# A stick-breaking attention stage with four softplus slots, its mask in the scores and its rounding on VectorE

## What is computed

```python
z = jnp.einsum("bhtd,bhsd->bhts", qb, kb) * scale
causal = s_idx < t_idx
log_not = jnp.where(causal, jax.nn.log_sigmoid(-z), 0.0)
tail = lax.cumsum(log_not, axis=3, reverse=True) - log_not
log_a = jax.nn.log_sigmoid(z) + tail
a = jnp.where(causal, jnp.exp(log_a), 0.0)
outs.append(jnp.einsum("bhts,bhsd->bhtd", a, vb))
```

## Time and profile before

| what | us |
|---|---|
| median of the three runs | 2361.65 |
| the profiled execution's own time | 2363.2 |
| its span, first to last instruction | 2361.4 |
| around the span | 1.8 |
| TensorE busy | 2258.7 |
| VectorE busy | 976.8 |
| ScalarE busy | 841.4 |
| GpSimd busy | 975.1 |

### The profile page before, as it was taken

How to read it: one execution, slowest core, us unless ns; L and a number is a source line. 1 busy time by engine, 2 the same in 40 slices (tenths; PEclk the granted TensorE clock), 3 DMA queues, 4 the chain that set the end, 5 groups by cost and what they waited for, 6 DMA issues and landing times.

```text
span 2361.4 us, 28298 instructions
## 1 busy us (share of the span) xinstructions
PE 2258.7 (96%) x10366; PEld 1781.8 (75%) x10366; DVE 976.8 (41%) x1433; ACT 841.4 (36%) x1410; POOL 975.1 (41%) x435
## 2 busy tenths in 40 slices
PE   8999999998889899999999999999999789999997
PEld 6888887874446688888777888888877458888886
DVE  3112347356674511134675421124552663211344
ACT  4222235323663422223443332222342763322222
POOL 4444444551002544444453354444443433544442
PEclk9999999998889999999999999999999989999999
DMA  5222332331001132223232232222222002322222
GB/s 184 89 106 89 107 107 89 125 125 36 1 1 38 70 107 89 107 89 118 78 107 72 90 107 91 104 89 107 80 95 76 19 1 72 122 92 93 103 89 71
DMA packets 29801, 202.67 MB, mean 86 GB/s; under 512 B 3360, under 2 KB 4000, under 8 KB 6048
## 3 DMA queue, kind: packets, MB, share of 16 engines
q1 hardware_dynamic: 28800, 198.55, 23.9%
q10 hardware_dynamic: 928, 3.14, 0.4%
HBM read 198.54 MB, written 2.10 MB: 85 GB/s over the span
## 4 chain that ended last, share of the span: by engine, by line
PE 87%; DVE 5%; ACT 4%; issue 2%; POOL 1%; ACTq 0%; DVEq 0%; POOLq 0%
PE PS L947 26%; PE PS L949 26%; PE PS L948 26%; PE PS L1270 1%; PE PS L1239 1%; DVE ACC L1430 1%; PE PS L1374 1%; PE PS L1198 1%; PE PS L1362 1%; DVE TMP L1510 1%; DVE NMAX L1662 1%; POOL X L471 1%; PE PS L1018 1%; PE PS L1094 0%; DVE PB L1681 0%
## 5 line engine op out<-in xcount | busy, mean ns | idle before, releaser
L446 POOL TENSOR_TENSOR WL<-RAW,WH 128x1024 fp32r<-128x1024 f32 x368 | 908.8, 2473 | 1276.0 <-ACT WH L512 1276.0
L947 PE MATMUL PS<-XH,WH 128*128 128x512 f32 (+1 forms) x2200 | 866.9, 394 | 30.4 <-DVE XL L1422 20.9
L949 PE MATMUL PS<-XH,WL 128*128 128x512 f32 (+1 forms) x2200 | 853.4, 388 | 0.0
L948 PE MATMUL PS<-XL,WH 128*128 128x512 f32 (+1 forms) x2200 | 853.1, 388 | 0.0
L512 ACT ACTIVATE WH<-RAW 128x1024 fp32r<-128x1024 f32 x368 | 388.1, 1059 | 1262.2 <-PE PS L949 1218.3
L947 PEld LDWEIGHTS PS<-XH,WH 128*128 128x128 f32 x2200 | 415.3, 189 | 126.6 <-issue 27.5
L948 PEld LDWEIGHTS PS<-XL,WH 128*128 128x128 f32 x2200 | 415.7, 189 | 85.8 <-issue 4.1
L949 PEld LDWEIGHTS PS<-XH,WL 128*128 128x128 f32 x2200 | 415.1, 189 | 84.8
L949 PE MATMUL PS<-HH,WL 128*128 128x512 f32 x672 | 261.7, 389 | 0.0
L948 PE MATMUL PS<-HL,WH 128*128 128x512 f32 x672 | 261.7, 389 | 0.0
L947 PE MATMUL PS<-HH,WH 128*128 128x512 f32 x672 | 261.7, 389 | 0.0
(11 more groups left out here) (194 smaller groups left out, 1639.3 us busy)
## 6 DMA issues: line engine op xcount, KB each, us to landing
RAW<-wstream SPq DMA_DIRECT2D x183, 1024.0 KB, 4.8
X<-xT SPq DMA_DIRECT2D x4, 512.0 KB, 9.4
WORK<-memT ACTq DMA_DIRECT2D x2, 1024.0 KB, 5.5
outT<-WORK SPq DMA_DIRECT2D x8, 256.0 KB, 2.1
RAW<-wstream SPq DMA_DIRECT2D x2, 512.0 KB, 6.5
PB<-WORK ACTq DMA_DIRECT2D x8, 127.8 KB, 2.4
CST<-consts SPq DMA_DIRECT2D x1, 912.0 KB, 12.1
WORK<-constsb SPq DMA_DIRECT2D x1, 256.0 KB, 12.7
```

Source lines behind the costliest of these rows:

```text
L446: pool.tensor_tensor(WL[:, s, :, :].rearrange("p a b -> p (a b)"), RAW[:, s, :], WH[:, s, :, :].rearrange("p a b -> p (a b)").bitcast(F), ...
L947: pe.matmul(o, wh, xh, start=start, stop=False)
L948: pe.matmul(o, wh, xl, start=False, stop=False)
L949: return pe.matmul(o, wl, xh, start=False, stop=stop)
```

## The change

The additive mask of the diagonal block moves from the end of the tail to just behind the scores of the pair (`sb_strict`), and VectorE's multiplication with the mask goes. The softplus is -1e30 clipped, so 0, where masked. The softplus has four slots in place of two, two of them in a new SBUF tensor `LT`. The rounding leaves ScalarE: VectorE makes the same maximum a second time, now written as fp32r into `XH`, two steps behind the clip; the unrounded maximum stays one step behind. The steps of every other round put their `XH` and `XL` columns at another place of the slot (`sb_cols`: 128 or 256 columns on for the two narrow widths), so that the rounding waits for a tail of one or two rounds before instead of the tail two steps before.

```diff
@@ -278,6 +278,7 @@
         VC = sb("VC", [32, P])
         EPSB = sb("EPSB", [P, 1])
         RSTDM = sb("RSTDM", [P, M])
+        LT = sb("LT", [P, 2, S])
         PS = ctx.enter_context(nc.psum_tensor("PS", [P, 8, S], F))
 
 
@@ -287,6 +288,7 @@
         V_WIN = W[:, 19, :].rearrange("p (t c) -> p t c", t=NT)
         V_SB = W[:, 14:20, :].rearrange("p a b -> p (a b)").rearrange("p (t c) -> p t c", t=NT)
         ASLOT = [PB[:, 2, :], PB[:, 3, :], W[:, 20, :], W[:, 21, :]]
+        LSLOT = [PB[:, 0, :], PB[:, 1, :], LT[:, 0, :], LT[:, 1, :]]
         ESLOT = [PT[:, 0, :], PT[:, 1, :], TMP[:, 0, :], TMP[:, 1, :]]
 
         PSLOT = [PB[:, m, :] for m in range(4)] + [W[:, 20, :], W[:, 21, :], Y0[:, :], ACC[:, :]]
@@ -376,6 +378,11 @@
         sums_ready = sem("sums_ready")
         out_ready, stored = sem("out_ready"), sem("stored")
 
+        def sb_cols(t, width):
+
+            at = (t // 8 % 2) * (P, 2 * P, 0, 0)[t % 8 // 2]
+            return slice(at, at + width)
+
         SBSTEPS = [(2 * c + r, j) for c in range(6) for j in range(NT - 1, -1, -1) for r in range(2)]
 
         def y_wait(eng, part, k):
@@ -478,7 +485,8 @@
                 for t, (h, j) in enumerate(SBSTEPS):
                     w = S - j * P
                     pool.wait_ge(sb_hi, t + 1)
-                    pool.tensor_tensor(XL[:, t % 8, 0:w], PB[:, t % 2, 0:w], XH[:, t % 8, 0:w].bitcast(F),
+                    pool.tensor_tensor(XL[:, t % 8, sb_cols(t, w)], LSLOT[t % 4][:, 0:w],
+                                       XH[:, t % 8, sb_cols(t, w)].bitcast(F),
                                        ALU.subtract).then_inc(sb_lo, 1)
 
 
@@ -906,14 +914,6 @@
                 act.wait_ge(sb_exp, t + 1)
                 act.activation(e, e, ACT.Ln, bias=1.0).then_inc(sb_ln, 1)
 
-            def sb_round(t):
-
-                w = S - SBSTEPS[t][1] * P
-                act.wait_ge(sb_l, t + 1)
-                if t >= 8:
-                    act.wait_ge(sb_tri, t - 1)
-                act.activation(XH[:, t % 8, 0:w], PB[:, t % 2, 0:w], ACT.Copy).then_inc(sb_hi, 1)
-
             def sb_weights(t):
                 w = S - SBSTEPS[t][1] * P
                 act.wait_ge(sb_tri, t + 1)
@@ -926,8 +926,6 @@
                     sb_weights(t - LAG_T)
                 if t < n:
                     sb_exp_ln(t)
-                if 1 <= t <= n:
-                    sb_round(t - 1)
             round_o(OUT_ORDER["outB"], lambda k: act.wait_ge(sb_o, k + 1) if k < 6 else
                     act.wait_ge(o_taken, 10 + k - 5))
             refill("outB", KC - 1)
@@ -1360,7 +1358,11 @@
                     pe.wait_ge(sb_a, (t | 1) - SBANKS + 1)
                 r = slice(DH * (h % 2), DH * (h % 2) + DH)
                 pe.matmul(PS[:, t % SBANKS, 0:S - j * P], W[r, 8 + h // 2, j * P:(j + 1) * P],
-                          Q[r, h // 2, j * P:S], start=True, stop=True).then_inc(sb_qk, 1)
+                          Q[r, h // 2, j * P:S], start=True, stop=False, skip_group_check=True)
+
+            def sb_strict(t):
+                pe.matmul(PS[:, t % SBANKS, 0:P], IDB, CSB[:, B_STRICT:B_STRICT + P], start=False, stop=False,
+                          skip_group_check=True).then_inc(sb_qk, 1)
 
             def sb_tail(t):
 
@@ -1371,10 +1373,9 @@
                 for n in range(NT - j):
                     col, width, m = n * P, w - n * P, SUMS[:, 1 if n == 0 else 0, :]
                     for part in (XH, XL):
-                        pe.matmul(bank[:, col:w], m, part[:, (t - 2 * n) % 8, 0:width], start=False,
-                                  stop=False, skip_group_check=True)
-                pe.matmul(bank[:, 0:P], IDB, CSB[:, B_STRICT:B_STRICT + P], start=False, stop=True,
-                          skip_group_check=True).then_inc(sb_tri, 1)
+                        mm = pe.matmul(bank[:, col:w], m, part[:, (t - 2 * n) % 8, sb_cols(t - 2 * n, width)], start=False,
+                                       stop=n == NT - j - 1 and part is XL, skip_group_check=True)
+                mm.then_inc(sb_tri, 1)
 
             def sb_values(t):
                 h, j = SBSTEPS[t]
@@ -1392,6 +1393,8 @@
                 if t < n:
                     sb_scores(t)
                     sb_scores(t + 1)
+                    sb_strict(t)
+                    sb_strict(t + 1)
                 if 0 <= t - LAG_T < n:
                     sb_tail(t - LAG_T)
                     sb_tail(t + 1 - LAG_T)
@@ -1803,7 +1806,7 @@
                 w = S - SBSTEPS[t][1] * P
                 dve.wait_ge(sb_qk, t + 1)
                 if t >= 4:
-                    dve.wait_ge(sb_l, t - 3)
+                    dve.wait_ge(sb_hi, t - 3)
                 dve.tensor_scalar(ESLOT[t % 4][:, 0:w], PS[:, t % SBANKS, 0:w], SPW, None,
                                   ALU.min).then_inc(sb_clip, 1)
 
@@ -1811,15 +1814,27 @@
 
                 w = S - SBSTEPS[t][1] * P
                 dve.wait_ge(sb_ln, t + 1)
-                if t >= 2:
-                    dve.wait_ge(sb_lo, t - 1)
-                lt = PB[:, t % 2, :]
-                chain(dve.tensor_tensor(lt[:, 0:w], ESLOT[t % 4][:, 0:w], PS[:, t % SBANKS, 0:w], ALU.max))
-                dve.tensor_tensor(lt[:, 0:P], lt[:, 0:P], CST[:, K_MASK:K_MASK + P], ALU.mult).then_inc(sb_l, 1)
+                if t >= 4:
+                    dve.wait_ge(sb_lo, t - 3)
+                lt = LSLOT[t % 4]
+                dve.tensor_tensor(lt[:, 0:w], ESLOT[t % 4][:, 0:w], PS[:, t % SBANKS, 0:w],
+                                  ALU.max).then_inc(sb_l, 1)
+
+            def sb_round(t):
+
+                w = S - SBSTEPS[t][1] * P
+                dve.wait_ge(sb_ln, t + 1)
+                c = t // 8 - (t % 8 < 4)
+                if c > 0:
+                    dve.wait_ge(sb_tri, 8 * c - 1 + t % 2)
+                dve.tensor_tensor(XH[:, t % 8, sb_cols(t, w)], ESLOT[t % 4][:, 0:w], PS[:, t % SBANKS, 0:w],
+                                  ALU.max).then_inc(sb_hi, 1)
 
             for t in range(n + LAG_V + 3):
                 if t < n:
                     sb_clip_(t)
+                if 2 <= t <= n + 1:
+                    sb_round(t - 2)
                 if 1 <= t <= n:
                     sb_soft(t - 1)
                 d = t - LAG_V - 1
```

## The result

The change made the kernel faster: 2343.16 us median of 8 runs (2338.72 to 2351.60) against 2360.43 us median of 8 for the kernel before. The ratio is 0.9929, 95% interval 0.9915 to 0.9943, so 16.8 us (13.5 to 20.1) came off where 11.2 were forecast. The time lies in the forecast range, 2341.5 to 2358.5. The kernel timed a second time beside the last experiments had 2346.73 us and a ratio of 0.9921 (0.9907 to 0.9935). Among the experiments one execution, of e6_scalar_no_turns, took 5978.67 us; its ratio leaves it out, and its cause is not known.

What follows compares the result with a forecast made beforehand. Bound: a loop of waits between TensorE's scores and first tail and ScalarE's queue. Saving 1.86 us a round, times 6, 11.2 us: profiled 2363.2 to 2352.0, and 2350.5 because that execution lay 1.55 above the median; range 2341.5 to 2358.5.

Steps and rivals of the forecast that it cites:

- Part 1: ScalarE's queue: two roundings leave each period, saving 2.96 us per round; the rounding's wait for the tail adds nothing.
- Part 2: TensorE: two mask matmuls before the first tail where one stood at its end, costing 0.24 us per round.
- Part 3: VectorE: mask multiplication (26.3 us) goes, second maxima (23 us) come at the first's price; SBUF operands judged dearer.
- Part 4: GpSimd's low part, behind VectorE's fuller queue, reaches the second tail of width 384 late by 0.72 us per round.
- Part 5: ScalarE's exp waits for a later clip in the period of the 384 scores: late by 0.14 us.
- Sum per round: Net saving of the stage per round: 2.96 - 0.24 - 0.72 - 0.14 = 1.86 us.
- Ends: Beginning and end of the stage together lose roundings from their chains, put at one more round's saving.
- Rival A: Denser work keeps TensorE's clock up, and the low part's lateness may not come: 2342.5 us; chance 0.2.
- B: VectorE's queue becomes the bound, second maxima held while GpSimd works; 7 us less saving, 2357.5 us; chance 0.16.
- C: TensorE's clock falls for most of the stage, costing 22.5 us: 2373 us; chance 0.04.
- D: Roundings were not on the loop; another wait takes over, gaining at most 2 us: 2360 us; chance 0.05.
- The signs: Profile marks of a right forecast: forecast periods, ScalarE back to back, stage about 96 us for 107, rest of span unchanged.

Runs made afterwards that it cites:

- e6_scalar_no_turns: e1_round_scalar without the turned columns and their looser wait, so ScalarE's rounding waits for the tail two steps before; 2360.17 us, ratio 0.9992.
- e7_copy_later: The changed kernel with VectorE's copy of a round's values one step later, behind the pair's second rounding; 2339.74 us, one execution.
- e5_mask_only: The kernel before with only the mask added behind the scores and VectorE's mask multiplication gone; 2360.09 us, ratio 0.9987.
- e1_round_scalar: The changed kernel with the rounding back on ScalarE, as a Copy from the softplus slot, keeping the looser wait; 2349.63 us, ratio 0.9936.
- after_again: The changed kernel itself, unedited, timed and profiled again beside e11_all; 2346.73 us, ratio 0.9921.
- e3_two_slots: The changed kernel with two softplus slots in place of four; 2344.80 us, one execution.
- e11_all: The changed kernel with rounding as VectorE's copy from SBUF, values' copy one step later, both weights of a pair before exp and ln; 2338.83 us, ratio 0.9894.

## Why the prediction was right, and where it was off

The forecast mechanism is what happened: a loop of TensorE's first tail and ScalarE's queue sets the periods, and it became shorter by the roundings that left it. One step failed without spoiling the number: the wait of the rounding for the tail, which the prediction put at nothing, was worth about half of what it booked under the roundings. By its steps:

*Part 1, two roundings leave each period, 2.96 us a round.* As the sum it holds (its first term is 1.07 and not 1.06, which changes nothing): 2.30 us came off net, and 0.5 to 0.6 were given back as lateness. As an account of what the roundings cost it fails. I wrote that the wait of the rounding for the tail was worth nothing beyond its queue time. In fact that wait is what put the first rounding on the loop: without it ScalarE does the first one in idle time, 15.32 us a round instead of 16.86. Taking the roundings off ScalarE is worth the rest, 0.77 us net, or 1.28 if the lateness that the move brings is taken out as well (15.32 to the 14.04 of e7_copy_later). The looser wait and the move both take the same first rounding off the loop, so they don't add, and the turns add nothing to the move (14.55 with and without).

*Part 2, masks ahead of the tail, 0.24 us a round.* Mis-sized: 0.0 net of the multiplication, from e5_mask_only, and 0.02 a period by the rows of e6_scalar_no_turns.

*Part 3, second maximum at the price of the first.* Right: 0.278, 0.410, 0.545 and 0.678 us for the four widths. That the SBUF form would be dearer was wrong for the copy: the row of 0.547 us read for it is an average over multiplications that were free (0.29) and held.

*Part 4, the low part late by 0.72 us in the period of the 128 scores.* Right in place and cause, a little too large: 0.49 us of wait; when the cause goes the period shortens by 0.6 and the round by 0.5. The low part ended 5.69 us after the 512 scores (5.94 forecast), and the second tail was ready for it at about 5.26 (5.22). VectorE's first clip came earlier than I had put it: in the changed kernel's period of the 512 scores, which start at 1867.75 us, it stood at 1.33 us, not 1.49:

```profile
1869.08 0.69 DVE L1810 TENSOR_SCALAR TMP<-PS 128x512 f32<-128x512 f32 x1 [0.74 <-PE PS L1364]
```

*Part 5, exp late by 0.14 in the period of the 384 scores.* That period lost 0.52 us of the 0.63 of its roundings, so about 0.1. Right.

*Sum per round.* 1.86 forecast, 2.30 to 2.38 measured (16.85 to 16.94 less 14.55). The excess is part 2 (0.24) and part 4 (about 0.2, from 0.72 to 0.51 net). Of the 15.39 us of the five rounds 12.3 are this, with the shorter first one: five full-clock rounds before are 84.3 to 84.7 us, after they took 72.17. I had put 9.3.

*Ends.* 1.86 forecast, 0.41 + 1.41 = 1.82 measured. The forecast was a round's saving taken over and not worked out, so the agreement is in part luck.

*Rival A, the clock.* The remaining 3.1 us of the 15.39 are rounds of the kernel before that the clock made longer: 87.56 us in place of 84.5. In the changed kernel the clock was 1.00 there, which is the sign that the prediction had set for A, and 2343.16 us lies nearer to A's 2342.5 than to 2350.5. But the clock is only 3.1 us of the 7: A came true in part, beside the forecast, and not through the absence of the lateness. What kept the clock is open. Over 1835 to 1915 us it was 0.97 to 1.00 in the nine profiles with a round of 14.6 us or less, 0.94 in e1_round_scalar (15.32), and below that it does not follow the round: 0.89 before, 0.87 with the mask alone, 0.86 with the turns alone (15.88), 0.84 in e6_scalar_no_turns. Those are single executions, nothing was done to the clock by itself, and the dips in after_again and e3_two_slots (rounds of 15.99 and 16.01 us) show that the changed kernel isn't free of them. The page "TensorE: Matmul & The Clock Gate" of the Trainium skill, Part 1, says that activity releases the throttle; the step from 0.84 to 0.89 up to 0.97 to 1.00 agrees with it in direction, the order within the slower four does not show it.

*Rivals B, C and D.* B: no second maximum was held, and between the waiting pairs the tails waited for GpSimd in one period only; the 0.7 us a round that B took for the hold was not worked out. C: the clock rose. D: the roundings, or their wait, were on the loop.

*The signs.* The periods forecast as 3.8, 4.3, 3.1 and 3.8 us were 3.61, 4.19, 3.01 and 3.74, and the rest of the span was unchanged. Two signs did not come: ScalarE is not back to back from the tail's end to the next scores (0.42 us idle ahead of the second weights), and the stage took 90.6 us and not about 96.

The time was 7 us below the forecast. By the two profiles 3.0 of that are the rounds, 3.1 the clock, and 1.1 lies before the stage and is the difference between two executions.

## What to carry to other kernels

A wait of an instruction in a strict queue has a price of its own, apart from the instruction: it decides whether the work stands behind the event on the loop or in the idle time ahead of it. Before moving an instruction to another engine, look at what it waits for; two edits that take the same instruction off the loop don't add, and here two of the four parts of the change, the slots and the turned columns, bought nothing beside the others. Before taking an average as a price, look whether its instructions are alike. The order in a queue can be worth as much as a move to another engine (0.77 us net here): one copy moved by one step and two weights drawn together were worth 1.0 us of a 14.55 us round together with a cheaper copy, and no part of the work was removed for it.

## What was not expected of the hardware

A free VectorE copy of fp32 from SBUF took 0.284 us at 256 columns and 0.351 at 384, where a maximum with one operand in PSUM took 0.410 and 0.545. Beside GpSimd's subtraction the copy can be held, the maximum was not (0.678 us on average at 512 columns, with subtractions running beside it). How much a copy is held depends on how its time falls against GpSimd's: in e11_all one copy of width 512 took 0.42 us and the next 0.92, and copies of width 128 took 1.00 and 0.21. And the length of the same kernel goes with the clock: over 35 executions of the kernel before, 2355.7 to 2368.3 us, a mean granted clock lower by 0.001 went with 1.3 us more.
